# Two transformer blocks on one core: one more one-hot on VectorE, written in pairs; the first query tiles in two steps; the identity loaded ahead

## The reference, cut to what matters

```python
q = (xb @ w_query).reshape(tb, 8, 2, 128)            # 8 heads, two halves
s = einsum('thpd,hpnd->thpn', q, sub_keys)           # scores of 2 x 128 keys
top_s, top_i = top_k(s, 16)                          # per half
best_s, pos = top_k(top_s[0] + top_s[1], 16)         # of 256 pairs
eid = top_i[0] * 128 + top_i[1]                      # 16 of 16384 experts a head
gate = softmax(best_s)
act = gelu(einsum('thkd,td->thk', expert_down[eid], xb))
out = einsum('thk,thkd->td', gate * act, expert_up[eid])
```

## Time and profile before

| | |
|---|---|
| profiled execution, device time | 3450.64 us |
| its span | 3448.8 us |
| TensorE matmul busy | 3270.0 us (95%) |
| VectorE busy | 2237.7 us (65%) |
| ScalarE busy | 1210.2 us (35%) |
| GpSimd busy | 833.4 us (24%) |
| granted TensorE clock, mean | 0.98 |

### The profile page before, as it was taken

One profiled execution on the slowest core, in us unless ns is written; L12 is line 12 of the kernel. 1 busy time (PEld: TensorE's weight loads), 2 busy tenths in 40 slices (PEclk: granted clock), 3 DMA queues, 4 the chain that ended last, 5 costly groups with the idle time before them and its releaser, 6 DMA issues.

```text
span 3448.8 us, 48108 instructions
## 1 busy us (share of the span) xinstructions
PE 3270.0 (95%) x16200; PEld 1958.9 (57%) x16200; DVE 2237.7 (65%) x4848; ACT 1210.2 (35%) x3239; POOL 833.4 (24%) x686
## 2 busy tenths in 40 slices
PE   8989998899999999989999899999899999999996
PEld 4445557656666666655445444445755666666664
DVE  1064598998887776772134400169899878777677
ACT  1141105886555550011021100110589545555001
POOL 0000043433333333420000000014343333333332
PEclk9999999999999999989998999999999999999998
DMA  4153227999999999982211122222799999999997
GB/s 153 74 195 148 84 76 269 357 413 395 418 416 411 401 403 420 421 353 82 85 49 55 49 73 73 73 98 81 283 359 410 398 408 411 413 401 402 418 414 315
DMA packets 129964, 927.42 MB, mean 269 GB/s; under 512 B 14848, under 2 KB 15744, under 8 KB 18208
## 3 DMA queue, kind: packets, MB, share of 16 engines
q0 software_dynamic: 73728, 536.90, 38.1%
q1 hardware_dynamic: 52416, 377.51, 27.6%
q10 hardware_dynamic: 3680, 11.36, 0.9%
HBM read 923.59 MB, written 2.12 MB: 268 GB/s over the span
## 4 chain that ended last, share of the span: by engine, by line
PE 55%; DMA 15%; issue 9%; DVE 8%; ACT 1%; DVEq 1%; POOL 1%; POOLq 0%; ACTq 0%
PE proj L545 18%; DMA ring<-in_experts,idx 15%; PE proj L800 14%; PE obk L791 7%; PE proj L537 5%; PE proj L725 4%; PE tps L754 3%; DVE xn L1652 3%; DVE ring L1635 3%; PE proj L861 1%; PE obk L901 1%; POOL ring L453 1%; ACT hT L1153 1%; DVE hT L1680 0%; PE obk L702 0%
## 5 line engine op out<-in xcount | busy, mean ns | idle before, releaser
L453 POOL DMA_INDIRECT ring<-in_experts,idx x512 | 688.7, 1345 | 1243.6 <-DVE xn L1652 1134.3
L800 PE MATMUL proj<-wring,hT 128*128 128x512 f32 x2048 | 952.1, 608 | 19.8 <-DVE hT L1694 17.3
L1635 DVE SCALAR_TENSOR_TENSOR ring<-ring,xn 128x1024 f32<-128x1024 f32 x512 | 609.0, 1221 | 173.9 <-DMA ring<-in_experts,idx 173.3
L791 PE MATMUL obk<-hT,wring 128*128 128x256 f32 x3072 | 694.2, 379 | 0.0
L791 PEld LDWEIGHTS obk<-hT,wring 128*128 128x128 f32 x3072 | 583.5, 190 | 159.5 <-issue 87.5
L1652 DVE SCALAR_TENSOR_TENSOR xn<-ring,coef,xn 128x1024 f32<-128x1024 f32 x512 | 628.7, 1280 | 20.4 <-DVE coef L1642 0.3
L800 PEld LDWEIGHTS proj<-wring,hT 128*128 128x128 f32 x2048 | 378.0, 192 | 405.5 <-issue 377.2
L1144 ACT ACTIVATE hot<-iotab,away 128x128 bf16<-128x128 bf16 x1856 | 567.3, 391 | 0.1
L545 PE MATMUL proj<-hT,wring 128*128 128x512 f32 x1216 | 530.6, 594 | 2.4 <-ACT hT L995 1.4
L545 PEld LDWEIGHTS proj<-hT,wring 128*128 128x128 f32 x1216 | 230.1, 191 | 283.2 <-issue 280.8
L474 POOL TENSOR_TENSOR ring<-ring 128x2048 bf16<-128x2048 bf16 x14 | 56.8, 4059 | 1311.5 <-DVE ring L1595 1311.5
(11 more groups left out here) (267 smaller groups left out, 2142.5 us busy)
## 6 DMA issues: line engine op xcount, KB each, us to landing
wring<-in_slabs SPq DMA_DIRECT2D x356, 1024.0 KB
ring<-in_experts,idx POOLq DMA_INDIRECT x512
x_res<-in_x SPq DMA_DIRECT2D x4, 512.0 KB, 7.8
ring<-in_keys ACTq DMA_DIRECT2D x2, 1024.0 KB, 9.7
out<-x_res SPq DMA_DIRECT2D x4, 512.0 KB, 2.6
ring<-ada_rows ACTq DMA_DIRECT2D x1, 1536.0 KB, 6.5
ring<-in_norm_pre ACTq DMA_DIRECT2D x2, 512.0 KB, 6.3
ring<-ada_rows ACTq DMA_DIRECT2D x1, 1024.0 KB, 19.2
```

The costliest lines, as they stand in the source:

```text
L453: pool.indirect_dma_start(rows[:, r, :], None, d[f"experts{layer + 1}"], bass.IndirectOffsetOnAxis(idx[:, k, r:r + 1], 0)).then_inc(row[r] ...
L791: m = pe.matmul(obk[:, j % 2, 0:DT], wring[:, k, at + c * P:at + (c + 1) * P], hT[:, c, GB * P:T], start=(c == 0), stop=(c == DC - 1))
L800: m = pe.matmul(proj[:, 2 * b + c, :], coefs[:, b * P:(b + 1) * P], wring[:, k, at + c * 512:at + (c + 1) * 512], start=False, stop=False, ...
L1635: v.scalar_tensor_tensor(rows[:, r, 0:D], rows[:, r, 0:D], 1.0, xn[:, r % GB, :], ALU.mult, ALU.mult, accum_out=dots[:, r:r + 1]).then_inc ...
```

## The change

Four things, with the same results computed:

- `ON_DVE` goes from 3 to 4. In the first pass VectorE makes four of eight `hot2` rows in one instruction, in a paired layout (tokens 2t and 2t+1 alternate element by element, `paired2`, a view on the same memory). TensorE loads those four as stationary operand with a step of two elements. ScalarE makes four rows in place of five.
- `route` computes the tiles of head 0 first for the tokens of blocks 0 to 2 (384 columns), then transposes block 3, then computes the last 128 columns. Before it waited for all four blocks.
- `all_read` stands behind these tiles instead of ahead of them.
- `ident` is loaded ahead of `gain1` and has a semaphore of its own; TensorE's first transposes wait for it alone, and not for `iota`.

```diff
-ON_DVE = 3
+ON_DVE = 4
...
+        paired2 = hot2.rearrange("p k (t u) n -> p k t (u n)", u=2).rearrange("p k t (n u) -> p k t n u", u=2)
...
-            pe.wait_ge(in_cst, 32)
+            pe.wait_ge(in_ident, 16)
...
-            for tb in range(1, TB):
+            for tb in range(1, TB - 1):
                 block_transposes(TR_F1, 1, tb)
-            def route(layer, first):
+            def route(layer, first, job, norm):
+                half_landed(2 * first % 4, 2 * first // 4)
+                for blocks in (range(TB - 1), range(TB - 1, TB)):
+                    at = slice(blocks[0] * P, (blocks[-1] + 1) * P)
+                    if blocks[0]:
+                        block_transposes(job, norm, TB - 1)
+                    pe.wait_ge(tr_free, job + 2 * (blocks[-1] + 1))
+                    for m in range(2):
+                        bank_free(4 * first + m)
+                        for c in range(DC):
+                            w = (m * DC + c) * P
+                            i = pe.matmul(proj[:, m, at], wring[:, 0, w:w + P], hT[:, c, at], start=(c == 0), stop=(c == DC - 1))
+                        if blocks[0]:
+                            i.then_inc(mm_done, 1)
                 all_read(first)
                 pe.wait_ge(in_keys, 16 * (layer + 1))
...
-                for h in range(PH):
+                key_scores(0)
+                for h in range(1, PH):
...
-            def spread_group(grp, k):
+            def spread_group(grp, k, pairs=0):
...
-                        m = pe.matmul(tps[:, k, t * CK:(t + 1) * CK], hot2[:, k, t, :], hot1[:, c, k, t // 2, :, t % 2],
+                        m = pe.matmul(tps[:, k, t * CK:(t + 1) * CK], paired2[:, k, t // 2, :, t % 2] if t < pairs else hot2[:, k, t, :],
+                                      hot1[:, c, k, t // 2, :, t % 2],
                                       start=(c == 0), stop=(c == PARTS - 1))
...
-                    spread_group(g + layer * CHUNKS * SGROUPS, g % 2)
+                    spread_group(g + layer * CHUNKS * SGROUPS, g % 2, ON_DVE)
...
-            pe.wait_ge(tr_free, TR_F1 + 8)
-            route(0, S_WQ1)
+            route(0, S_WQ1, TR_F1, 1)
...
-            block_transposes(TR_F2, 3, TB - 1)
-            pe.wait_ge(tr_free, TR_F2 + 8)
-            route(1, S_WQ2)
+            route(1, S_WQ2, TR_F2, 3)
...
-            for t, n in ((gain1, "attn_norm_g"),):
-                act.dma_start(t, d[n]).then_inc(in_g1, 16)
-            for t, n in ((ident[:, :], "ident"), (iota, "iota")):
-                act.dma_start(t, d[n]).then_inc(in_cst, 16)
+            act.dma_start(ident[:, :], d["ident"]).then_inc(in_ident, 16)
+            act.dma_start(gain1, d["attn_norm_g"]).then_inc(in_g1, 16)
+            act.dma_start(iota, d["iota"]).then_inc(in_cst, 16)
...
-                    some = [P, ON_DVE, NK]
-                    v.tensor_tensor(hot2[:, k, 0:ON_DVE, :], bcast(iotab[:, :], 1, some),
-                                    bcast(keys[:, 1, bass.ds(token, ON_DVE)], 2, some), ALU.is_equal)
+                    some = [P, ON_DVE // 2, NK, 2]
+                    v.tensor_tensor(paired2[:, k, 0:ON_DVE // 2, :, :], bcast(iota2[:, :, :], 1, some),
+                                    bcast(keys[:, 1, bass.ds(token, ON_DVE)].rearrange("p (t u) -> p t u", u=2), 2, some), ALU.is_equal)
```

More of the change, by code:

```diff
@@ L307, in build @@
         in_x = [sem(f"in_x{tb}") for tb in range(TB)]
-        in_cst, in_g1, in_blk1 = sem("in_cst"), sem("in_g1"), sem("in_blk1")
+        in_cst, in_ident, in_g1, in_blk1 = sem("in_cst"), sem("in_ident"), sem("in_g1"), sem("in_blk1")
         sq_done, b_arg, z_ready = sem("sq_done"), sem("b_arg"), sem("z_ready")
@@ L1393, in _ @@
                 normed(tb + 1, tb, gain1).then_inc(xn_ready, 1)
-            v.wait_ge(in_cst, 32)
+            v.wait_ge(in_cst, 16)
+            v.wait_ge(in_ident, 16)
             v.tensor_copy(iota2[:, :, :], bcast(iota, 2, [P, NK, 2]))
```

## The result

The changed kernel took 3428.43 us (median of nine runs, 3420.44 to 3432.86) beside 3450.47 of the kernel before (nine runs, 3438.13 to 3458.42). The ratio is 0.9938, with a 95% interval of 0.9929 to 0.9948: 22.0 us or 0.6% faster. Forecast were 3435 (3424 to 3449) and a gain of 15.2. So the time lies inside the range and the gain 6.8 above the forecast one. The span of the profiled execution is 3426.6.

A forecast was written before the change was run, and what follows sets the result against it. TensorE was taken to bound most of the chain (55%), VectorE alone without a gap in the first spread pass. Gains 1.4 + 0.4 + 4.1 + 8.6 + 0.7 = 15.2 gave about 3435 us, range 3424 to 3449.

The forecast's parts named there:

- Part 1, the start: Start of kernel: with the identity first, TensorE starts between 8.9 and 9.4 instead of 10.59; gain 1.2 to 1.7, taken 1.4.
- no later than both did together, 8.1: Start: the gain vector, now second in the queue, lands by 8.1, when identity and gain vector were both there before.
- Part 2, layer 1: Layer 1's routing opening: query tiles in two steps bring key scores sooner; gain 0.4, bounds -0.2 to 0.5.
- Part 3, layer 2: Layer 2's routing opening: the same split fills TensorE's 7.79 idle stretch; gain 4.1, with 2.5 lost to the clock's fall.
- Part 4, the spread: First spread pass, both layers: four paired one-hots on VectorE save 0.135 a group over 64 groups; gain 8.6, bounds 17 to 0.
- the seam: End of the first spread pass: VectorE's wait of 1.4 for the last copy shrinks; 0.3 a layer, 0.7 in all.
- the line between 256 and 768: Spread pass: 512 paired elements priced at 0.335, between 0.20 for 256 paired and 0.47 for 768 paired.
- Transfers take the gain: Rival, spread pass: DMA share already 0.96, so only 5.9 of the gain remain, 3444.5 us; chance 0.12.
- Unpaired pace: Rival, spread pass: the new VectorE instruction takes 0.61 like the unpaired one, losing 9, 3453.5 us; chance 0.05.
- Strided loads slow: Rival, spread pass: TensorE's 12 stepped loads a group take 110 ns each and bind, 3474 us; chance 0.07.
- The late half: Rival, layer 2's routing: the first half-slab lands as late as rows allow; part 3 loses 2.7, 3442 us; chance 0.06.
- The clock holds, or falls briefly: Rival, layer 2's routing: TensorE's clock holds or falls only briefly, 2.5 more gained, 3432.5 us; chance 0.15.

The follow-up runs named there:

- the control: The kernel before, unchanged, built and timed as if it were another: 3447.02 us, ratio 1.0003.
- the spread alone: Only four paired one-hots on VectorE, on the kernel before, timed twice: 3437.37 us (ratio 0.9984) and 3434.04 us (0.9963).
- the earlier request: Changed kernel, layer 2's first query half-slabs requested one output tile sooner: 3424.3 us (0.9945); also with the gain vector loaded before the identity: 3423.53 us (0.9940).

## Why the prediction was right, step by step

**Part 1, the start: forecast 1.4, found 0.8 on average.** The mechanism was right: TensorE waits for VectorE and no longer for `iota`. But the bound "no later than both did together, 8.1" for the gain vector was wrong: it landed at 7.9 or at 9.0. In the seven traces with the new order TensorE starts at 9.4 to 9.6 five times and at 10.6 twice. The step took the two landings of the earlier trace rows for fixed times of the queue.

**Part 2, layer 1: forecast 0.4, found 0.3, and something beside it.** The products took 10.39 (369.79 to 380.18) where 10.3 were expected, the turn 1.78 where it was 1.83, the small ones 3.67 where it was 3.5. (The prediction's own sum ends at 388.6, and it goes on with 388.7; by the rows it shows the gain is 0.5.) The split opening is 17.02 long in all nine traces that have it. The unsplit one is 17.3 in two traces and 19.0 in three (in the control, and in both of the spread alone), where the 32 products take 15.70 in place of 14.00. The first of the spread alone (timeline, then windows with columns as in the earlier trace rows):

```profile
373.10 15.70 PE L546 MATMUL proj<-hT,wring 128*128 128x512 f32 x32 [0.74 <-ACT hT L997]
```

```profile
374.00:375.00 1.00, 1.00 (x2) 0.34 (x2) 1.00 (x1) 0.00 (x0) 0.00 (x0) 0.50 0.00 0
```

The clock is at 0.50 from 373.6 to 377.0 there. So the split saves 1.3 on average over these few traces. The reading of one execution couldn't show that, and the prediction had no term for it.

**Part 3, layer 2: forecast 4.1, found 3.7 on average.** In the first trace it was 2.9: the half landed 4.9 and not 4.4 behind its request, and the cold products cost 3.0 and not 2.5. In the later ones of the changed kernel request to key scores is 22.4, just under the 22.6 forecast. There the clock is back sooner, as the windows of the last trace show:

```profile
2252.00:2255.00 3.00, 2.80 (x5) 1.60 (x6) 1.68 (x3) 1.18 (x3) 0.00 (x0) 0.56 1.02 431
2255.00:2257.00 2.00, 2.00 (x7) 1.16 (x6) 0.99 (x1) 0.00 (x0) 0.00 (x0) 0.81 1.00 422
2257.00:2260.00 3.00, 3.00 (x11) 1.80 (x10) 0.00 (x0) 0.00 (x0) 0.00 (x0) 1.00 0.63 265
```

So in three of seven traces the clock was low for half as long (3.4 in place of 6.8). Over the seven traces with the split and the request of before, it is 22.4 three times and 23.7 four times; over five without the split, 26.6 to 27.1. The clock's price is so 1.7 (12.28 - 10.56) or 3.0; the taken 2.5 lies between.

**Part 4, the spread: forecast 8.6 and 0.7 at the seam, found 9.3.** 0.34 against 0.335 on the line between 256 and 768, four groups in 11.34 against 11.33 (593.16 to 604.50), the loads unchanged. 32 x 0.135 = 4.3 a layer; the pass went from 94.42 to 89.77, 4.65. The remaining 0.3 is the seam: VectorE waits 0.37 there in the control (above) and not at all in the kernel after (timeline):

```profile
649.45 0.39 ACT L1149 ACTIVATE ring<-tps 128x256 f32<-128x256 f32 x1 [0.21 <-PE tps L770]
649.89 1.10 DVE L1700 TENSOR_TENSOR hT<-ring 128x256 f32<-128x256 f32 x2
```

That the seam's term came out is luck in part: the wait of 1.4 in the earlier trace rows, from which it was argued, was for the most part the odd execution's, and the real one, 0.37, happened to be hardly longer than the 0.3 that was taken. VectorE has no wait between 560 and 650 in the kernel after, as the prediction asked.

**The sum.** 0.8 + 1.3 + 3.7 + 9.3 = 15.1, against 15.2 forecast and 22.0, 17.2 and 15.0 measured (mean 18.1). That the sum fits so well is luck: 0.6 too much in part 1 and 0.4 in part 3 stand against 0.9 too little in part 2. The prediction gave a gain of over 0.5% a chance of only 0.36, and it came in two comparisons of three by the ratio. About 3 of the mean have no step, and I call them open. The traces show where such time lies: behind the first pass of layer 2, from its first coefficients to the last row sum. That stretch takes 879.5 to 880.4 in the three traces of the changed kernel and 883.1 and 883.2 in the two of the kernel before; over all fourteen it is 879.5 to 882.4 wherever the pass is the shorter one, and 882.1 to 885.7 elsewhere. What makes it shorter wasn't tested. The three intervals reach 3.3 to 5.7 to either side, and the traces wander by as much where nothing is changed: two of the changed kernel reach layer 1's first row dot at 560.1 and at 563.6, and the second block's mixer, from its convolution to the request of the query slabs, takes 704.8 to 710.0 over six traces of the kernel before and of its single parts.

**The rivals.** *Transfers take the gain*: no. From the last coefficients of layer 1's second pass (781.4 before, 771.4 after) to the last dense sum of TensorE in that layer it took 747.2 before and 746.1 after, and layer 2's later passes didn't grow either (above): nothing was given back. The transfers did fit, with a DMA share of 0.94 from 564 to 649 in place of 0.92. *Unpaired pace*: 512 unpaired elements take 0.60, near the 0.61 priced (384 in 0.47 would have made it 0.63), but the new ones aren't unpaired. *Strided loads slow*: no, 0.75 with half of the loads stepped and 0.77 with none (above). The Trainium skill, TensorE: Matmul & The Clock Gate, section on Fast Weight Load, names strided columns beside packed ones as fit for the quick load; the rows agree, 24 loads and products in 0.75 with half of them stepped. *The late half*: no; it landed 4.9 behind its request. *The clock holds, or falls briefly*: it never held in the changed kernel or its variants with the request of before; it fell for the shorter time in three of seven traces, and held in both with the earlier request.

## What to carry to other kernels

When an engine without a gap bounds a stage, price its instructions by the distance to their successor, each layout on its own line: pairing the innermost dimension took this comparison from 0.60 to 0.34 for 512 elements and the pass from 98.0 to 89.8, while the split with two on VectorE, paired too, stands at 98.1. When a wait on a transfer is removed, look at which transfer lands next: here the one moved back in the queue became the new wait. And before a stall of one microsecond in one trace becomes a term, see it in a second trace of the same code.

## What of the hardware was not expected

The same load of 512 KB, issued second at 1.20, landed at 7.8 to 8.0 in five executions and at 9.0 in two others. At an unchanged seam ScalarE took up the last copy 0.34 or 1.37 behind its releaser, in both layers of one execution alike. And a stretch of 32 products, behind three short idle stretches of TensorE (1.30, 1.23 and 0.74), ran either wholly at full clock (14.00, two traces) or lost 1.70 (15.70, three), with the same instructions each time; the split version of it, behind two (1.30 and 0.78), lost nothing in nine.
